# FFN first halves of a two-part transformer block stack: weights stationary and 256 tokens moving from the second block on

## What is computed

```python
def swiglu(x, w_in, w_out):
    gate, up = jnp.split(x @ w_in, 2, axis=-1)
    return (jax.nn.silu(gate) * up) @ w_out

# first part, twice in each of four layers (g: a gain of norm_g)
h = h + 0.5 * rms_norm(swiglu(rms_norm(h, g[0]), w_in, w_out), g[1])

def rms_norm(x, g, eps=1e-6):
    y = x * lax.rsqrt(jnp.mean(x * x, axis=-1, keepdims=True) + eps)
    return y * g

# second part, once in each of two layers: no norm behind the FFN, but a modulation ahead
h2 = modulate(rmsnorm(x, norm2[l]), sh2, sc2)
gate, up = jnp.split(h2 @ w_ffn_in[l], 2, axis=-1)
x = x + g2 * ((jax.nn.silu(gate) * up) @ w_ffn_out[l])
```

## Time and profile before

| | us |
|---|---|
| median of 3 runs | 2811.11 (2810.86 to 2811.58) |
| span of the profiled execution | 2808.9 |
| median less span | 2.2 |
| TensorE busy | 2777.8 (99%) |
| weight loads busy | 2268.2 (81%) |
| VectorE busy | 1855.1 (66%) |
| ScalarE busy | 1538.8 (55%) |

### The profile page before, as it was taken

One profiled execution on the slowest core, in us unless ns is written; L12 is line 12 of the kernel. 1 busy time (PEld: TensorE's weight loads), 2 busy tenths in 40 slices (PEclk: granted clock), 3 DMA queues, 4 the chain that ended last, 5 costly groups with the idle time before them and its releaser, 6 DMA issues.

```text
span 2808.9 us, 34710 instructions
## 1 busy us (share of the span) xinstructions
PE 2777.8 (99%) x13354; PEld 2268.2 (81%) x13354; DVE 1855.1 (66%) x2704; ACT 1538.8 (55%) x2662; POOL 186.7 (7%) x300
## 2 busy tenths in 40 slices
PE   8999999999999999999999999999999999999998
PEld 7888788888888888886888888788788788788787
DVE  6766776676667667667676776667754755745754
ACT  6547754654665465467654645765454544444543
POOL 1000100000000010015001001110000000000000
PEclk9999999999999999999999999999999999999999
DMA  7765467566536756651666675367665565654652
GB/s 260 236 210 190 143 211 254 188 225 225 187 126 213 254 188 212 238 205 54 195 225 226 216 249 207 110 216 234 213 218 195 187 203 190 211 194 165 208 182 105
DMA packets 358660, 559.40 MB, mean 199 GB/s; under 512 B 15680, under 2 KB 245056, under 8 KB 358240
## 3 DMA queue, kind: packets, MB, share of 16 engines
q1 hardware_dynamic: 350752, 535.02, 56.4%
q0 software_dynamic: 7600, 21.81, 2.3%
q10 hardware_dynamic: 144, 0.36, 0.0%
HBM read 556.03 MB, written 1.10 MB: 198 GB/s over the span
## 4 chain that ended last, share of the span: by engine, by line
PE 95%; DVE 2%; ACT 1%; issue 1%; DMA 0%; POOL 0%; SPq 0%; DVEq 0%; ACTq 0%
PE ps L703 40%; PE ps L793 27%; PE ps L709 20%; PE ps L673 4%; PE ps L874 1%; PE ps L905 1%; ACT SB L1593 1%; PE ps L762 1%; ACT JUNK L1441 0%; PE ps L915 0%; PE ps L882 0%; DVE M L2005 0%; DMA RAW<-in_ffn_w_in 0%; PE ps L850 0%; PE ps L1053 0%
## 5 line engine op out<-in xcount | busy, mean ns | idle before, releaser
L703 PE MATMUL ps<-HI,XH 128*128 128x512 f32 x2480 | 983.3, 396 | 3.2 <-DVE LO L1865 2.4
L703 PE MATMUL ps<-LO,XH 128*128 128x512 f32 x2480 | 967.9, 390 | 0.0
L1860 DVE TENSOR_TENSOR LO<-RAW,HI 128x1024 fp32r<-128x1024 f32 x468 | 568.8, 1223 | 342.4 <-ACT HI L1421 338.3
L709 PE MATMUL ps<-HI,XL 128*128 128x512 f32 x2480 | 767.6, 391 | 0.4
L1865 DVE SCALAR_TENSOR_TENSOR LO<-RAW,GC,HI 128x512 fp32r<-128x512 f32 (+1 forms) x896 | 623.5, 746 | 189.1 <-ACT HI L1428 186.7
L1421 ACT ACTIVATE HI<-RAW 128x1024 fp32r<-128x1024 f32 x468 | 492.4, 1059 | 450.5 <-PE ps L793 296.0
L1428 ACT ACTIVATE HI<-RAW,GC 128x512 fp32r<-128x512 f32 (+1 forms) x896 | 587.7, 714 | 152.2 <-PE ps L709 126.9
L709 PEld LDWEIGHTS ps<-HI,XL 128*128 128x128 f32 x2480 | 463.6, 188 | 107.8 <-DVE XL L1901 9.7
L703 PEld LDWEIGHTS ps<-HI,XH 128*128 128x128 f32 x2480 | 466.0, 188 | 100.7 <-DVE LO L1865 3.6
L703 PEld LDWEIGHTS ps<-LO,XH 128*128 128x128 f32 x2480 | 466.1, 188 | 92.0
L793 PE MATMUL ps<-HI,AH 128*128 128x512 f32 x856 | 266.3, 392 | 0.0
(11 more groups left out here) (221 smaller groups left out, 2085.6 us busy)
## 6 DMA issues: line engine op xcount, KB each, us to landing
RAW<-in_ffn_w_in SPq DMA_DIRECT2D x350, 512.0 KB, 4.6
RAW<-in_ffn_w_out SPq DMA_DIRECT2D x88, 1024.0 KB, 4.9
RAW<-in_w_ada SPq DMA_DIRECT2D x48, 1024.0 KB, 5.0
RAW<-in_w_in SPq DMA_DIRECT2D x44, 1024.0 KB, 5.0
RAW<-in_w_ffn_in SPq DMA_DIRECT2D x88, 512.0 KB, 4.6
RAW<-in_diff_w_in SPq DMA_DIRECT2D x24, 1024.0 KB, 5.0
RAW<-in_w_ffn_out SPq DMA_DIRECT2D x22, 1024.0 KB, 4.9
RAW<-in_moba_w_in SPq DMA_DIRECT2D x12, 1024.0 KB, 5.0
```

What stands on the lines that cost most here:

```text
L703: e.matmul(ps[:, b + t, 0:nw], XH[:, k, t * P:(t + 1) * P], q[s][:, c * nw:(c + 1) * nw], start=(k == 0 and q is HI), stop=False)
L709: i = e.matmul(ps[:, b + t, 0:nw], XL[:, k, t * P:(t + 1) * P], HI[s][:, c * nw:(c + 1) * nw], start=False, stop=(k == 7))
L1860: e.tensor_tensor(LO[n % NSPLIT][:, 0:w], RAW[t.buf][:, at[1] * w:(at[1] + 1) * w], HI[n % NSPLIT][:, 0:w].bitcast(F32), ALU.subtract).the ...
```

## The change

From the second block on of each FFN's first half, `features_by` takes the place of `tokens_by`: the weights are stationary, 128 features at a time (`j`), and the 256 tokens move. The result has features on partitions: bank b holds the gate's 256 features as two groups of 256 tokens, bank b + 1 the up features. AF needs no turn there, so AH is copied from AF in SBUF and AL made from AF in SBUF. The first block stays as it was and is turned by `first_turned`.

With features on partitions the root is no number of a partition any more. In folded steps two transposes of the roots, each repeated over 128 columns, give a row of 256 (`roots_turned`, in bank 5), which ScalarE copies to RB. VectorE multiplies the gate by RB into SG (`s_gr`), ScalarE applies Silu to SG in place, and VectorE multiplies by up. The up side gets no root at all, in the first block neither: the next norm takes that factor out, and its eps is made to fit by two GpSimd operations on one column (`eps_of`).

```diff
+                def first_turned():
+                    e.wait_ge(s_af, c["af"] + 1)
+                    turn(ps[:, 4, :], [AF[:, 0, t, j * P:(j + 1) * P] for j in range(2) for t in range(2)]
                          ).then_inc(s_tf, 1)
+                def roots_turned():
+                    for t in range(2):
+                        r, n = root_of(st, t)
+                        e.wait_ge(s_pw, n)
+                        i = e.transpose(ps[:, 5, t * P:(t + 1) * P], r.to_broadcast([P, P]), ident)
+                    i.then_inc(s_rbt, 1)
+                def features_by(n, k2, b):
+                    s = n % NSPLIT
+                    quarters = [(c, gu, j) for c in range(2) for gu in range(2) for j in range(2)]
+                    for c, gu, j in quarters:
+                        for x in (XH, XL):
+                            e.matmul(ps[:, b + gu, j * S:(j + 1) * S], HI[s][:, c * 512 + gu * S + j * P:][:, 0:P],
+                                     x[:, 2 * k2 + c, :], start=(k2 + c + j == 0 and x is XH), stop=False,
+                                     skip_group_check=True)
+                    for c, gu, j in quarters:
+                        i = e.matmul(ps[:, b + gu, j * S:(j + 1) * S], LO[s][:, c * 512 + gu * S + j * P:][:, 0:P],
+                                     XH[:, 2 * k2 + c, :], start=False, stop=(2 * k2 + c == 7), skip_group_check=True)
+                    return i
...
                     for k2 in range(4):
-                        if k2 == 2:
-                            activations_turned(jp - 1, 4)
+                        if jp == 1 and k2 == 2:
+                            if st.fold:
+                                roots_turned()
+                            first_turned()
                         n = st.w0 + 4 * jp + k2
                         taken(n)
-                        for t in range(2):
-                            i = tokens_by(n, k2, t, b, 512, None, None)
-                        i.then_inc(s_used, 1)
+                        features_by(n, k2, b).then_inc(s_used, 1)
                 def ready(k, t):
-                    if (k, t) == (0, 0):
-                        e.wait_ge(s_al, c["al"] + JP - 1)
-                    elif (k, t) == (FC - 2, 0):
-                        e.wait_ge(s_al, c["al"] + JP)
+                    if t == 0 and k % 2 == 0:
+                        e.wait_ge(s_al, c["al"] + k // 2 + 1)
...
# ScalarE, in the loop over blocks
+                        if jp == 1 and st.fold:
+                            e.wait_ge(s_rbt, c["rbt"] + 1)
+                            e.activation(RB[:, :], ps[:, 5, 0:S], ACT.Copy).then_inc(s_rb, 1)
+                        activations_high(jp - 1)
                         split(st.w0 + 4 * jp + 9)
+                    if st.fold and jp >= 1:
+                        e.wait_ge(s_gr, c["gr"] + jp)
+                        e.activation(SG[:, i], SG[:, i], ACT.Silu).then_inc(s_sg, 1)
+                        continue
...
# VectorE, in the loop over blocks
+                    if st.fold and jp >= 1:
+                        if jp == 1:
+                            e.wait_ge(s_rb, c["rb"] + 1)
+                        e.wait_ge(s_used, st.w0 + 4 * jp + 4)
+                        e.tensor_tensor(SG[:, i], ps[:, b, :].rearrange("p (j n) -> p j n", j=2),
+                                        RB[:, :].unsqueeze(1).to_broadcast([P, 2, S]), ALU.mult).then_inc(s_gr, 1)
                     e.wait_ge(s_sg, c["sg"] + jp + 1)
                     if jp >= 2:
-                        e.wait_ge(s_tf, c["tf"] + jp - 1)
-                    if st.fold:
-                        for t in range(2):
-                            o = e.scalar_tensor_tensor(out=AF[:, i, t], in0=ps[:, b + t, S:2 * S], scalar=root_of(st, t)[0],
-                                                       in1=SG[:, i, t], op0=ALU.mult, op1=ALU.mult)
-                        o.then_inc(s_af, 1)
+                        e.wait_ge(s_ah, c["ah"] + jp - 1)
+                    up = ps[:, b:b + 2, S:2 * S] if jp == 0 else ps[:, b + 1, :].rearrange("p (j n) -> p j n", j=2)
+                    e.tensor_tensor(AF[:, i], SG[:, i], up, ALU.mult).then_inc(s_af, 1)
```

More of the change, by code:

```diff
@@ L327, in build @@
         s_al = sem("s_al")
+        s_rbt = sem("s_rbt")
+        s_rb = sem("s_rb")
+        s_gr = sem("s_gr")
+        s_ep = sem("s_ep")
         s_tf = sem("s_tf")
@@ L1530, in ffn, with activations_high @@
                 c = st.c
-                AH, SG = st.t["AH"], st.t["SG"]
+                AH, SG, AF, RB = (st.t[x] for x in ("AH", "SG", "AF", "RB"))
                 second_rows(st)
[L1534 to L1537, removed]
+                def activations_high(jp):
+                    if jp == 0:
+                        e.wait_ge(s_tf, c["tf"] + 1)
+                        src = ps[:, 4, :].rearrange("p (j n) -> p j n", j=2)
+                    else:
+                        e.wait_ge(s_af, c["af"] + jp + 1)
+                        src = AF[:, jp % 2]
+                    e.activation(AH[:, 2 * jp:2 * jp + 2, :], src, ACT.Copy).then_inc(s_ah, 1)
                 for jp in range(JP):
@@ L1556, in ffn @@
                         o.then_inc(s_sg, 1)
-                    else:
-                        e.activation(SG[:, i], ps[:, b:b + 2, 0:S], ACT.Silu).then_inc(s_sg, 1)
-                activations_high(JP - 1, 2)
+                    elif jp == 0:
+                        e.activation(SG[:, i], ps[:, b:b + 2, 0:S], ACT.Silu).then_inc(s_sg, 1)
+                    else:
+                        e.activation(SG[:, i], ps[:, b, :].rearrange("p (j n) -> p j n", j=2), ACT.Silu).then_inc(s_sg, 1)
+                split(st.w0 + 4 * JP + 6)
+                activations_high(JP - 1)
                 split(st.w1 + 2)
@@ L1913, in by_gain @@
                 s0, s1, v = stats_of(b.k, t)[:3]
+                eps = 1e-6
+                if steps[b.k - 1].kind == "ffn":
+                    eps, n = eps_of(steps[b.k - 1], t)
+                    e.wait_ge(s_ep, n)
                 e.wait_ge(s_g[b.g1.buf], 16 * b.g1.turn)
@@ L2508, in folded @@
                     root(r2, v2)
+                if steps[b.k].kind == "ffn":
+                    for t in range(2):
+                        e.tensor_scalar(eps_of(steps[b.k], t)[0], stats_of(b.k, t)[6], 1e-6, None, ALU.mult).then_inc(s_ep, 1)
             def phase(st):
```

34 lines of the change are left out of this document (15 added, 19 removed).

## The result

The changed kernel takes 2828.27 us (median of 4 runs, 2827.89 to 2829.17), the kernel before 2811.07 us (4 runs, 2810.86 to 2811.58) beside it: a ratio of 1.0061, interval 1.0047 to 1.0075. It is 17.2 us slower. I had forecast 2802 us; rival C had 2827 us, with a chance of 0.24.

The account below looks back on a forecast made before the run. TensorE, busy 99% of 2808.9 us, was taken as the only bound. Terms of -50 + 39 + 1.8 + 0.3 = -9 us took 2811 us to 2802 us, with a range of 2762 to 2824 us.

Parts of the forecast that it names:

- rival C: FFN first halves: load exchange costs a fixed time, two varying streams, the later decides; 120 ns gives 2827 us; chance 0.24.
- What bounds the kernel: Whole kernel: TensorE alone, busy 99% of 2808.9 us; time is a number of matmuls times the distance between starts.
- -50 us for the transposes: FFN blocks from the second on: 100 groups of four AF transposes go, at 0.50 us each.
- +39 us for the narrow matmuls: FFN first halves: 9600 matmuls of 256 columns at the gates' 117.4 ns instead of 113.3 ns each.
- Rival B: FFN first halves: the 256-column stream settles at 113.3 to 116.8 ns; 2763 us at 113.3 ns; chance 0.30.
- Break-even at 118.5 ns: FFN first halves: distance per 256-column matmul at which 9600 of them cost the 50 us saved on transposes.
- +1.8 and +0.3 us: TensorE: 16 added transposes of roots in eight folded FFNs, +1.8 us; slow matmuls at ten seams to 512 columns, +0.3 us.
- Nothing elsewhere: VectorE, ScalarE, GpSimd, loads and queues: changed work there adds no time; VectorE 10.7 of about 11.3 us in ada blocks.
- D: Ada blocks: VectorE falls behind, a new wait of up to 1 us in 8 FFNs x 2 blocks; 2818 us; chance 0.03.

Follow-up runs that it names:

- e1: Kernel before, with the transposes of AF left out from the second block on (400 of 440): 2761.1 us, ratio 0.9821.
- e4: Changed kernel, with the gates' matmul order, 48-column weight slices and single PSUM region tried in different FFNs, alone or combined: 2820.3 us.
- e2: Kernel before, transposes kept and tokens stationary, each first-half matmul from the second block on split into two of 256 columns: 2869.21 us, ratio 1.0205.
- e7: Changed kernel, with HI and LO weight pieces 64 bytes further in their tiles, in first halves from the second block on: 2790.79 us, ratio 0.9927.
- e3: Kernel before, with the 512 columns of the second halves' matmuls cut into different widths from FFN to FFN: 2944.8 us.
- e9: e7 with the statistics columns (roots included) of even steps placed 384 bytes beyond those of odd steps: 2775.25 us, ratio 0.987.
- e6: Changed kernel, with XH and XL side by side so HI is loaded once for 512 columns and only LO has 256: 2792.8 us, ratio 0.9935.
- e5: Changed kernel, with all stationary slices shifted by 32 bytes more from FFN to FFN, 0 to 224 bytes, then again from 0: 2822.9 us.
- e8: Changed kernel with the tiles of e7, the weight pieces 128 bytes further instead of 64: 2826.27 us, ratio 1.0052.
- e10: e7 with the statistics columns (roots included) of odd steps placed 384 bytes beyond those of even steps: 2790.44 us, ratio 0.9926.

## Why the prediction was wrong, step by step

- **What bounds the kernel: right.** TensorE 99% busy before and after, the time is a count times a distance.
- **-50 us for the transposes: right**, by e1 alone (50.2), and in the count (40 transposes of AF are left). One of its readings was loose: 168 matmuls in 38.13 us are 227.0 ns each; the 226.7 is that of the 12 in 2.72 us and of the steady stream.
- **+39 us for the narrow matmuls: this step failed.** I took 117.4 ns from the gates "since ... it is a measurement of the same operand types and sizes". It was not one of the same operand starts. (By the nanosecond records the row is 117.6, which would be +41 us; the difference is rounding.) In the FFN it is 120.07 ns, which makes 9600 x (120.07 - 113.35) = +64.5 us. e4 shows why the row does not carry over: with slices in steps of 48 columns, and nothing else of the gates, the FFN has 117.58 too. I had the line with `m * 48` before me and did not hold it against the FFN's `j * P`.
- **Rival C: the right number for a wrong reason.** Its time (2827 us) was met. Its mechanism, two jittering streams of which the later decides, is refuted: 120 ns has no scatter, is the same with VectorE's and ScalarE's tiles stationary or moving (e2), and goes away by 64 bytes (e7). So meeting its time was luck. The part of its name that holds is the fixed cost, for slices at these starts: 13.3 ns per matmul (e3), so that twice as many matmuls pay it twice.
- **Rival B: wrong here, and possible.** The stream does settle, within two or three matmuls, but at 120. It settled at B's 113.3 only where the slices begin 64 bytes off, and there only behind some of the interruptions (e7, e9).
- **Break-even at 118.5 ns: fits.** No run lay on it, but the sum from which it comes holds within 1 us. By it e7's slow pace of 117.87 in all ten FFNs would be 2807 us (an estimate), just below the kernel before. The whole case hung on 1.5 ns per matmul.
- **+1.8 and +0.3 us: fit.** -50 + 64.5 + 1.8 + 0.3 = +16.6 us, against 17.2 measured; under 1 us is unaccounted for.
- **Nothing elsewhere, and D's 0.03: right.** VectorE in the ada block is busy 9.37 us, where I had worked out 10.7 (its terms add up to 10.6), and TensorE waits for no new name. Over the whole run it is busy 32 us longer, 0.3 us a block.

On the rule of the Trainium skill, "TensorE: Matmul & The Clock Gate", section "Back-to-back issue gap": its direction held, that narrow matmuls cost more per column. Its sizes, an estimate of 109.2 and 215.8 ns for 256 and 512 columns, were met by no fp32r stream here: the fastest steady ones are 113.3 and 226.7 ns. The page gives them for a matmul by itself and says that in a stream with a load before each matmul both set the distance; so they were no price for this stream, and the prediction did not say that.

What stays open: why the start of the stationary slice matters for the pace at all; why a stream of 256 columns at 64 bytes has two steady paces; and by which rule the address of an operand that is read once, 912 matmuls earlier, picks one. The starts in the text are counted from the tiles' own beginnings; no run moved the tiles of the moving operand and nothing else, so whether it is the slice's address alone or its distance to the moving rows' address was not tried. Nor was a fix for FFN 8 and 9, worth 2 x 912 x 4.5 ns = 8 us by the same sum.

## What to carry to other kernels

Where TensorE is the bound, price a matmul by the distance of starts in a long steady stretch with the same width, types and also the same operand starts; a row that agreed in width and types only was 2.6 ns off here, and 2.6 ns times 9600 (25 us) decided the sign of this change. Halving the width to get rid of transposes pays only if the fixed part of a matmul, here 13.3 ns for fp32r at the unshifted starts, costs less than they do; keeping one wide matmul over two operands side by side (e6) took back 35 of the 64 us. When a steady stream is some nanoseconds above its columns, shift the stationary slices by 64 bytes in one FFN at a time, as e5 does, before giving up the idea.

## What the runs showed of the hardware that I had not expected

- A stream of 256-column fp32r matmuls had steady distances of 113.3, 117.8 or 120.0 ns at one clock, types and order, depending on where its stationary slices begin and, at one start, on what came before (e5, e7, e8). For 512 columns the unshifted start was the best of eight: 226.8 to 227.7 ns against 229.8 to 235.0 (e5).
- The pace can be a state: the same stream goes on at 113.3 or at 117.8 ns for 912 matmuls, changing at an interruption by six transposes or not (e7), and moving the tile's columns that two of these read turned the slow one into the fast one (e9), though not the other way round (e10).
- A 128-column matmul with its own load takes 111.8 ns, hardly less than one of 256 with 120.6; by the fitted sums nothing is saved below some 237 columns (e3).
- Transposes interrupt narrow matmuls more cheaply than wide ones: a group of four cost 0.50 us among wide ones and 0.44 among narrow ones (e2).
